# A hybrid decoder step on one core: row-block start, paired feed-forward units and rotation on raw tiles

## The reference

```
z = rmsnorm(x, norm_mix) @ w_in                    # 1024 -> 6400: q, k, v, hgrn (4 x 512), pool, gates
q = rope(rmsnorm(zq, q_norm), pos); k = rope(rmsnorm(zk, k_norm), pos)   # heads of 64
o_b = windowed attention with sinks(q, k, v, cache)
o_a = hgrn2 recurrence;  o_c = multi-scale pooling
x = x + (sum_n sigmoid(zg_n) * (o_n @ w_branch_n)) @ w_o
x = x + relu(rmsnorm(x, norm_ffn) @ w_up)**2 @ w_down    # 1024 -> 4096 -> 1024
rope(x): [x1*cos - x2*sin, x2*cos + x1*sin]   with x1, x2 the halves of a head
```

## Time and profile before

| | |
|---|---|
| median of 3 runs | 949.89 us (949.81 to 949.96) |
| the profiled execution | 949.91 us |
| its span in the trace | 948.1 us |
| PE busy, share of the span | 943.3 us, 99% |
| DVE busy | 669.3 us, 71% |
| ACT busy | 483.8 us, 51% |
| transfers, mean | 173 GB/s |

### The profile page before, as it was taken

The page is one execution under the profiler, slowest core; times in us unless marked ns, Lnnn a source line. Parts: engine busy times, 40 slices in busy tenths (PEclk is TensorE's granted clock), DMA queues, the critical chain, the costliest instruction groups (busy, mean ns, idle before and its releaser), DMA issues.

```text
span 948.1 us, 18976 instructions
## 1 busy us (share of the span) xinstructions
PE 943.3 (99%) x7944; PEld 914.9 (96%) x7944; DVE 669.3 (71%) x1052; ACT 483.8 (51%) x707; POOL 43.2 (5%) x61
## 2 busy tenths in 40 slices
PE   9999999999999999999999999999999999999998
PEld 8999898999999999999999998989999999999998
DVE  6798798858876755555757887889498676556463
ACT  6429663473664353535553586436537644435351
POOL 0070000000000000000001500000000000000000
PEclk9999999999999999999999999999999999999999
DMA  9655444444554585455475563534444546555542
GB/s 361 219 186 172 184 145 134 135 134 152 156 182 153 192 300 176 156 172 161 162 253 164 189 219 113 166 123 147 135 145 156 182 147 244 172 163 172 160 155 91
DMA packets 44276, 164.25 MB, mean 173 GB/s; under 512 B 4992, under 2 KB 6528, under 8 KB 43648
## 3 DMA queue, kind: packets, MB, share of 16 engines
q1 hardware_dynamic: 42912, 152.95, 49.1%
q0 software_dynamic: 1136, 9.83, 2.7%
q10 hardware_dynamic: 144, 0.26, 0.1%
HBM read 153.29 MB, written 10.29 MB: 173 GB/s over the span
## 4 chain that ended last, share of the span: by engine, by line
PE 97%; DMA 1%; ACT 0%; SPq 0%; DVE 0%; issue 0%; DVEq 0%; ACTq 0%
PE pz L413 90%; PE pm L413 6%; DMA raw<-in_w 1%; PE pm L579 1%; ACT w_hi L783 0%; DVE arena L1022 0%; PE pm L632 0%; PE pm L642 0%; SPq L356 0%; SPq L350 0%; PE pm L531 0%; SPq L360 0%; DVE arena L1054 0%; DVE xp L1058 0%; ACT rstd L801 0%
## 5 line engine op out<-in xcount | busy, mean ns | idle before, releaser
L413 PE MATMUL pz<-a_hi,w_hi 128*128 128x288 f32 x1376 | 413.2, 300 | 0.9 <-DVE a_lo L1027 0.6
L413 PE MATMUL pz<-a_lo,w_hi 128*128 128x288 f32 x1376 | 405.9, 295 | 0.0
L413 PE MATMUL pz<-a_hi,w_lo 128*128 128x288 f32 x1376 | 404.8, 294 | 0.0
L783 ACT ACTIVATE w_hi<-raw 128x1024 fp32r<-128x1024 f32 x266 | 278.0, 1052 | 208.5 <-PE pz L413 196.7
L1013 DVE TENSOR_TENSOR w_lo<-raw,w_hi 128x1024 fp32r<-128x1024 f32 x266 | 327.4, 1231 | 10.8 <-ACT w_hi L783 10.8
L413 PEld LDWEIGHTS pz<-a_hi,w_hi 128*128 128x128 f32 x1376 | 257.9, 187 | 10.5 <-issue 8.6
L413 PEld LDWEIGHTS pz<-a_hi,w_lo 128*128 128x128 f32 x1376 | 259.0, 188 | 0.0
L413 PEld LDWEIGHTS pz<-a_lo,w_hi 128*128 128x128 f32 x1376 | 258.3, 188 | 0.3
L413 PE MATMUL pz<-h_hi,w_hi 128*128 128x288 f32 x768 | 228.2, 297 | 0.0
L413 PE MATMUL pz<-h_lo,w_hi 128*128 128x288 f32 x768 | 226.5, 295 | 0.0
L413 PE MATMUL pz<-h_hi,w_lo 128*128 128x288 f32 x768 | 225.8, 294 | 0.0
(11 more groups left out here) (175 smaller groups left out, 539.9 us busy)
## 6 DMA issues: line engine op xcount, KB each, us to landing
raw<-in_w SPq DMA_DIRECT2D x267, 512.0 KB, 3.5
arena<-in_s SPq DMA_DIRECT2D x2, 2048.0 KB, 9.6
out_ss_out<-arena POOLq DMA_DIRECT2D x2, 2048.0 KB, 8.1
out_u_out<-arena POOLq DMA_DIRECT2D x2, 864.0 KB, 6.8
arena<-arena SPq DMA_DIRECT2D x8, 180.0 KB, 3.2
arena<-in_kcT SPq DMA_DIRECT2D x2, 512.0 KB, 6.9
arena<-in_vc SPq DMA_DIRECT2D x2, 512.0 KB, 7.6
out_kc_out<-in_kc_kept POOLq DMA_DIRECT2D x1, 992.0 KB, 7.0
```

The costliest lines, as they stand in the source:

```text
L413: return nc.tensor.matmul(out, a, b, start=start, stop=stop, **kw)
L783: act_fn(w_hi[:, r], raw[:, r], ACT.Copy).then_inc(s["w_hi"], 1)
```

## The change

1. Start. The first three units are laid out in memory by row blocks: block k of all three units (384 columns) is one transfer, issued just before the piece of x with the same row block, in six pieces of one, one, one, one, two and two blocks. PE takes block after block over three banks (9 products each). Squares of x are made between the blocks, into eight buffers. WARM is 8 and FILL is gone.
2. Loads. The rest of the constants goes behind unit 5's load, the pool state behind unit 7's, the caches behind 14 and 15, the pool weights behind 16, the masks (POOL's queue) behind the read of tile 5.
3. Feed-forward. PE takes two units at a time, block by block, alternating between two banks (`pair`); single units remain at the first two steps of the first turn and from step SINGLE = 12 of the last. DVE makes the split of even steps at the step's beginning.
4. Rotation. The swapped copy is made of the raw q and k tiles (SP's step 9, after tile 4's read); DVE multiplies raw tiles by weight and cos (u = 5) and the copy by the swapped weight and sin (u = 6), adds, and multiplies by the norm's factor (u = 7).
5. Parameters. Two more columns a layer for the swapped weights, and the number of columns is rounded up to a multiple of 8, so the tensor of parameters and x grows from 96 + 2304 to 112 + 2304 columns.

The diff, cut to its core:

```diff
-WARM = 11
-FILL = 4
+WARM = 8
+SINGLE = 12
-X_PIECES = ((0, 1), (1, 4), (4, 6), (6, 8))
+PIECES = ((0, 1), (1, 2), (2, 3), (3, 4), (4, 6), (6, 8))
+FIRST = 3
+SQUARED = {2: (0, 2), 4: (2, 4)}
-NPAR = _at
+NPAR = (_at + 7) // 8 * 8
+        def raw_first(j0, j1):
+            return raw[:, 0:FIRST].rearrange("p u n -> p (u n)")[:, j0 * FIRST * P:j1 * FIRST * P]
+        def split_first(w, j0, j1):
+            return w[:, 0:FIRST, j0 * P:j1 * P].rearrange("p u (k c) -> p u k c", c=P)
...
-            for j0, j1 in X_PIECES:
-                if j0 == 4:
-                    sp.dma_start(raw[:, 0, 512:UW], io["w"][0][:, 512:UW]).then_inc(s["raw0_landed1"], 16)
+            for j0, j1 in PIECES:
+                if j0 > 0:
+                    sp.dma_start(raw_first(j0, j1), w_first(j0, j1)).then_inc(s[f"w_landed{j0}"], 16)
                 sp.dma_start(xp[:, piece], io["x_in"][:, piece]).then_inc(s[f"x_landed{j0}"], 16)
+            sp.dma_start(consts[:, 0:early], io["consts"][:, 0:early]).then_inc(s["consts_landed"], 16)
...
+                    if l == 0 and u == 5:
+                        sp.dma_start(consts[:, early:], io["consts"][:, early:]).then_inc(s["consts_rest"], 16)
-                    if u == 5:
+                    if u == 7:
                         sp.dma_start(uext[:, :, PAD + NP:], io["pool_state"][l]).then_inc(s["ustate_landed"], 16)
-                    if u == 6:
+                    if u == 14:
...
                         sp.dma_start(kcT, io["kcT"][l]).then_inc(s["cache_landed"], 16)
-                    if u == 7:
+                    if u == 15:
                         sp.dma_start(vc, io["vc"][l]).then_inc(s["cache_landed"], 16)
-                    if u == 13:
-                        sp.wait_ge(s["qk_norm"], 3 * l + 3)
+                    if u == 9:
+                        sp.wait_ge(s["z_read_dve"], read_dve(l, U_K))
...
+            def first_units():
+                for k in range(KT):
+                    i = [n for n, (j0, j1) in enumerate(PIECES) if j0 <= k][-1]
+                    pe.wait_ge(s["a_hi"], k + 1)
+                    if PIECES[i][0] == k:
+                        pe.wait_ge(s["w_first_hi"], i + 1)
+                    for n in range(FIRST):
+                        mm(outs[n], hi[n][:, k], a_hi[:, k], start=k == 0, stop=False)
+                    pe.wait_ge(s["a_lo"], k + 1)
+                    for n in range(FIRST):
+                        mm(outs[n], hi[n][:, k], a_lo[:, k], start=False, stop=False)
...
+            def pair(outs, g, rhs_hi, rhs_lo, have=None):
+                for k in range(KT):
+                    if have is not None:
+                        have(k)
+                    for n in range(2):
+                        mm(outs[n], hi[n][:, k], rhs_hi(k), start=k == 0, stop=False)
+                    for n in range(2):
+                        mm(outs[n], hi[n][:, k], rhs_lo(k), start=False, stop=False)
+                    for n in range(2):
+                        last = mm(outs[n], lo[n][:, k], rhs_hi(k), start=False, stop=k == KT - 1)
+                        if k == KT - 1:
+                            last.then_inc(s["unit_done"], 1)
...
+                for j in range(0, 16, 2):
+                    single = (first and j == 0) or (last and j >= SINGLE)
+                    for n in ((0, 1) if single else (1,)):
+                        pe.wait_ge(s["w_lo"], l * UNITS + i * 16 + (u + n + 1) + HEAD)
+                        pe.wait_ge(s["z_read_dve"], i * 16 + read_dve(l, T_FFN + j + n - 4))
...
+                        else:
+                            pair(outs, l * UNITS + u, rhs_hi, rhs_lo, have)
...
+            for j0, j1 in PIECES:
+                act.wait_ge(s[f"x_landed{j0}"], 16)
+                for j in range(j0, j1):
+                    input_hi(j, first_norm)
+                    if j == j0:
+                        act.wait_ge(s[f"w_landed{j0}"], 16)
+                        act_fn(split_first(w_hi, j0, j1), by_unit(raw_first(j0, j1)),
+                               ACT.Copy).then_inc(s["w_first_hi"], 1)
+                if j1 in SQUARED:
+                    for j in range(*SQUARED[j1]):
+                        square(1, j)
+            split(FIRST)
...
+                if u in (5, 6):
+                    src, turned, table, done = ((qk, "", cos, "qk_cos"), (sin_t, "_turned", sin, "qk_sin"))[u - 5]
...
+                    else:
+                        dve.wait_ge(s["qk_turned"], 64 * (l + 1))
+                    stt(dst[:, 0:4 * T].rearrange("p (j t) -> p j t", j=4), src[:, 0:4 * T].rearrange("p (j t) -> p j t", j=4),
+                        pr(l, "qw" + turned), bc(table, 4), ALU.mult, ALU.mult).then_inc(s[done], 1)
+                    stt(dst[:, 4 * T:5 * T], src[:, 4 * T:5 * T], pr(l, "kw" + turned), table, ALU.mult,
+                        ALU.mult).then_inc(s[done], 1)
                 if u == 7:
+                    tt(cos_t, cos_t, sin_t, ALU.add).then_inc(s["qk_turn"], 1)
...
+                    tt(qk[:, 0:3 * QR].rearrange("p (b n) -> p b n", b=3), cos_t[:, 0:3 * QR].rearrange("p (b n) -> p b n", b=3),
+                       pm[:, 0:3, 0:QR], ALU.mult).then_inc(s["qk_norm"], 1)
...
             def mlp(l, i, last, first=False):
                 for j in range(16):
+                    g = l * UNITS + U_FFN + i * 16 + j + LEAD
+                    early = j % 2 == 0 and not (i == 0 and j == 0) and not (last and j >= SINGLE)
+                    if early and g < DEPTH * UNITS:
+                        split(g)
...
-                    g = l * UNITS + U_FFN + i * 16 + j + LEAD
-                    if g < DEPTH * UNITS:
+                    if not early and g < DEPTH * UNITS:
                         split(g)
...
-            pool.wait_ge(s["consts_rest"], 16)
+            pool.wait_ge(s["z_read_dve"], read_dve(0, U_V))
             pool.dma_start(A[:, 4096:4096 + lmask.shape[1] * P], io["lmask"]).then_inc(s["lmask_landed"], 16)
```

More of the change, by code:

```diff
@@ L445, in first_have @@
                     def first_have(k):
[L446 to L456, removed]
+                        pe.wait_ge(s["a_lo"], l * 16 + (k + 1))
                     def third_have(k):
@@ L731, in new_state, with ffn_turn @@
                     mm(PM[h], ktok_s[rows], imask[rows, q:q + 4].rearrange("p b n -> p (b n)")).then_inc(s["snew"], 1)
-            def ffn_turn(l, i, first=False):
-                for j in range(16):
+            def ffn_turn(l, i, first, last):
+                for j in range(0, 16, 2):
                     u = U_FFN + j
-                    pe.wait_ge(s["w_lo"], l * UNITS + i * 16 + (u + 1) + HEAD)
-                    pe.wait_ge(s["z_read_dve"], i * 16 + read_dve(l, T_FFN + j - 4))
-                    out = [PZ[bank(l, T_FFN + j)][:, 0:T]]
+                    single = (first and j == 0) or (last and j >= SINGLE)
@@ L739, in ffn_turn @@
                     if j < 8:
-                        have = (lambda k: pe.wait_ge(s["a_lo"], l * 16 + (9 + k))) if first and j == 0 else None
-                        product(out, l * UNITS + u, lambda k: a_hi[:, k], lambda k: a_lo[:, k], KT, have)
-                    else:
-                        have = (lambda k: pe.wait_ge(s["f_lo"], l * 8 * FI + i * 8 + (k + 1) + HEAD)) if j == 8 else None
-                        product(out, l * UNITS + u, lambda k: h_hi[:, k], lambda k: h_lo[:, k], KT, have)
+                        rhs_hi, rhs_lo = (lambda k: a_hi[:, k]), (lambda k: a_lo[:, k])
+                    else:
+                        rhs_hi, rhs_lo = (lambda k: h_hi[:, k]), (lambda k: h_lo[:, k])
@@ L745, in ffn_turn @@
+                    have = None
                     if first and j == 0:
-                        norm_sum(2 * l + 2)
-                    if first and j in (7, 12):
-                        new_state(l, 0 if j == 7 else 4)
+                        have = lambda k: pe.wait_ge(s["a_lo"], l * 16 + (9 + k))
+                    if j == 8:
+                        have = lambda k: pe.wait_ge(s["f_lo"], l * 8 * FI + i * 8 + (k + 1) + HEAD)
+                    outs = [PZ[bank(l, T_FFN + j + n)][:, 0:T] for n in range(2)]
@@ new lines, in ffn_turn @@
+                    for n in ((0, 1) if single else (1,)):
+                        pe.wait_ge(s["w_lo"], l * UNITS + i * 16 + (u + n + 1) + HEAD)
+                        pe.wait_ge(s["z_read_dve"], i * 16 + read_dve(l, T_FFN + j + n - 4))
+                        if single:
+                            product(outs[n:n + 1], l * UNITS + u + n, rhs_hi, rhs_lo, KT, have)
+                            if first and j == 0 and n == 0:
+                                norm_sum(2 * l + 2)
+                                have = None
+                        else:
+                            pair(outs, l * UNITS + u, rhs_hi, rhs_lo, have)
@@ L750, in _ @@
+                    if first and j in (6, 12):
+                        new_state(l, 0 if j == 6 else 4)
             for name in ("unit_done", "nsum", "pool_y"):
@@ L794, in square @@
```

(8 more changed lines are left out.)

145 lines of the change are left out of this document (74 added, 71 removed).

## The result

The changed kernel takes 943.73 us (943.59 to 944.05, 6 runs) against 949.87 (949.75 to 950.16, 6 runs) for the kernel before beside it: a ratio of 0.9934 with the interval [0.9924, 0.9945], 6.1 us faster. The profiled execution took 943.61 us, its span is 941.8. What the prediction's sum put on the start came nearly as forecast; the rest, 5 us net, came from a part that the prediction had at zero, less what the pairs cost.

What follows compares the result with a forecast made beforehand. PE bounds the kernel, busy 943.3 of 948.1 us, mostly in one matmul helper at 0.1333 us a product. The start takes 1.3 us off the median 949.89, everything else zero: 948.6 us, range 946.4 to 950.9.

Steps and rivals of the forecast that it cites:

- Operands at multiples of 64 bytes: Input tensor grows by 64 bytes a partition: zero effect; a slower fetch would show on every product.
- Row blocks at the start: First three units by row blocks: fifth tile starts at 20.2 instead of 21.53, 1.3 us earlier; bounds 0.5 and 2.6.
- the wait at the fifth block: At the start, PE waits 0.6 us with a restart for ACT's 768-column split of the fifth block.
- the clock's bound: Shorter warm-up at the start: five real products still at the lower clock level, 0.6 us more; left out of the sum.
- The forecast's steps behind 17.7: After DVE's last sums at the start: norm sum 0.6, root and passes 0.95, tile 0's read 0.45; with signals 20.2.
- Feed-forward two by two: Bank changes in 2784 products cost nothing, at most 34 us either way; pairs' split margin: 0, at worst some tenths a layer.
- The last down pair of the first turn: Feed-forward: DVE's 6.1 us plus 0.3 drain against the pair's 6.4; forecast 0, at worst some tenths once a layer.
- the pairs starve: Rival, chance 0.12: PE waits before a pair for DVE's low half of its second unit; 951.8 to 954.4 us.
- alternation lifts the limit: Rival, chance 0.07: alternating banks in the feed-forward lifts the product's 0.133 us towards 0.121; down to 915 us.
- Loads, rotation: Moved loads cost nothing; rotation on raw tiles, DVE 7.5 us after, gains nothing; without cover up to 1 us a layer lost.
- the prediction's 30 us: By the skill page's 122.5 ns, an order lifting whatever stands between products would save 30 us; not counted.

Runs made afterwards that it cites:

- e1: Kernel before with 8 more unused parameter columns a layer, so its operands start 64 bytes later: 944.18 us against 949.92.
- e2: Changed kernel with 64 bytes a partition more of unused parameters, operands again at a multiple of 128 bytes: 947.96 us, ratio 0.9979.
- e3: Changed kernel with every feed-forward unit on its own, one bank per 24 products (pairs undone): 943.01 us, ratio 0.9927.
- e9: Changed kernel without pairs, the four operands as slices of one tensor beginning 12 bytes later (76 past a multiple of 256): 936.20 us, ratio 0.9858.
- maps: Stretches of 48 products behind the last unit of the kernel before, with operands, output, banks or columns varied: 133.33 ns at its own place, 132.22 at 64 bytes.
- e5: Finer map on the kernel before: moving operand shifted in steps of 4 bytes, weights in steps of 16; 133.31 ns at 0, 131.11 at 12 bytes.
- e4: First map on the kernel before: coarser shifts of operands and output, 256 to 512 columns, one or two banks; 133.33 ns with both operands moved by 64.
- e7: Changed kernel without pairs and without rounding the parameter count; operands landed 32 bytes past a multiple of 256, 16 was meant: 952.95 us, ratio 1.0030.
- e10: Changed kernel without pairs, operands 12 bytes later, rows of a and h in turn (76 and 204 past a multiple of 256): 930.86 us, ratio 0.9800.
- e11: Changed kernel without pairs, rows of a and h in turn, without the 12 bytes (64 and 192 past a multiple of 256): 946.63 us, ratio 0.9966.

## Why the prediction was wrong, step by step

**The step that failed** is "Operands at multiples of 64 bytes", put at zero because what lies behind the input tensor "keeps its place against such multiples". It does, and e1 and e2 show that such multiples are not what counts: 64 bytes take 1.1 ns off every product, some 5.7 us in all (e1), and 64 more bring the old time back to units that go alone (e2). The prediction named the sign to look for ("would show on every product") but only as a loss; a gain from this part was in no case of its range. No trace of a single placement could give the size, since all its products share two places. But the earlier trace rows held the question: 133.3 ns, where half of the pooling step's 242 for as many columns at two clocks each is 121. The rival that asked why it was 0.133 gave the answer to alternation alone; the measured time lies where that rival had it, by luck, for without the pairs it is lower still (e3).

**Row blocks at the start: right, its closeness in part luck.** 1.3 us forecast, 1.18 in the trace, 1.17 between the medians of e1 and e3. The first product came 0.2 us before its forecast and the wait at the fifth block was half its size; against that the clock's bound, not counted in the sum, came true in this trace, six products 0.24 us apart, 0.6 us. Unit 3 began at 16.41 (forecast 16.0), the fifth tile 0.16 us late. The forecast's steps behind 17.7 (0.6, 0.95 and 0.45) make 19.7; the 0.5 us of signals up to its 20.2 stand in no row. How many products run slow differs between executions of the same start: none of those behind the first in e2 and e3, eleven in e9.

**Feed-forward two by two.** That a change of bank costs and gives nothing was right (maps; e3). The price of the pairs was right in kind and wrong in place. The last down pair of the first turn, 6.4 against 6.4, held: the pair that waits for its splits, at 327.06 us, loses 0.07 us. The pair that stopped was the first, whose second split stands behind the norm's root on ACT; PE waits 0.27 us for it and loses 0.1 more at the restart; no step had costed it. That is the rival "the pairs starve", at a quarter of its price: 0.37 us a layer. The rival "alternation lifts the limit" fell at the changed kernel's place; at the old one the order of a pair saves 0.5 ns (e2).

**Loads, rotation.** No wait of PE for a rotated query, a cache or a mask stands in the list, as forecast. DVE's rotation takes 2 x (1.42 + 0.51) + 1.65 + 1.28 + 0.59 = 7.4 us (forecast 7.5). Against the earlier trace rows, the masks' cast now runs beside the rotation, and no split takes 2 us.

**The page.** "TensorE: Matmul & The Clock Gate" of the Trainium skill, section "Back-to-back issue gap", gives the formula behind 122.5 ns as that of an isolated gap, apart from streams in which each product has its own weight load, as here; so the prediction's 30 us were at most an estimate from another case. No run here shows 122.5, the shortest level is 130.0.

**The sum** as measured: 5.7 for the place (before to e1), 1.2 for the start (e1 to e3), 0.7 back for the pairs (e3 to the changed kernel): 6.2, against 6.1 between the medians. These are steps from one kernel to the next, so their sum has to come out; what each step consists of is read in its trace.

## What to carry to other kernels

Where one form of matmul fills the span, its start-to-start time is a term of every change that moves a tensor, even one that adds two columns of parameters: compare this time in both traces before looking for stages. A stretch of the same instruction behind the kernel's last unit, with the operands shifted in steps of 4 bytes, costs one run and gives the whole table; then choose the start and the row distance by it, and test the choice in the whole kernel, with the compiled addresses in hand, since a place can have two levels. Work that releases two buffers together needs its margin checked at the first group of a stage, not only at the tightest steady one.

## What the runs showed of the hardware

The time from one 288-column product to the next depends on where the moving operand starts, to 4 bytes, and on where the weights start (moved in steps of 16): 130.0 to 136.7 ns in the stretches of e5, 5%, at a granted clock of 1.00. It is not a matter of 288 columns: at 0 and 64 bytes, 256 columns take 118.4 and 115.9 ns, 384 take 175.6 and 173.6, 512 take 230.4 and 230.8 (e4). Moving either operand by 64 bytes shifts the level and moving both brings it back, but for finer moves it is not shown that only the difference counts (e5: weights moved by 48, 131.11, the moving operand by as much the other way, 132.61). The pattern over the starts nearly repeats after 128 bytes when rows alternate by 128 (e5: 131.11 at 12 and at 140, 133.31 and 133.28 at 0 and 128). The best starts of the moving operand are mostly those 12 past a multiple of 16; of the weights' moves the four 48 past a multiple of 64 have 131.1 to 131.2. Why is open: no run here looks below the start times, and a cause was not tried. Nor is it settled what chooses between two levels where a place has two: 133.3 and 134.4 in e7, 130.0 and 133.3 in e10, 131.65 and 132.2 in e11. The changed kernel's start also shows products 0.24 us apart for six products while the clock's column reads 1.00; that column does not tell the two rates apart here.
